# Twenty places instead of eighteen for the expert weights of a hybrid-attention and mixture-of-experts block

## What is computed

```python
h = x
h = h + hybrid_mixer(rms_norm(h, norm_mix_g), w_in, q_norm_g, k_norm_g, w_proj_a, w_proj_b, w_out, cos, sin)
hn = rms_norm(h, norm_ffn_g)
h = h + moe_ffn(hn, w_router, b_router, w_gate_up, b_gate_up, w_down, b_down)

# moe_ffn: 32 experts, the 4 best of a token by the router's logits, gates = softmax over these 4;
# for each expert e and the tokens xb that chose it:
hgu = xb @ w_gu[e] + b_gu[e]                          # 1024 x 2048
gate, up = min(hgu[:, :1024], 7), clip(hgu[:, 1024:], -7, 7)
y = ((up + 1) * gate * sigmoid(1.702 * gate)) @ w_down[e] + b_down[e]   # 1024 x 1024
```

## Time and profile before

| | |
|---|---|
| median of 3 runs | 1224.87 us (1224.17 to 1225.32) |
| the profiled execution's own time | 1224.58 us |
| span of its trace | 1223.0 us |
| PE busy | 1146.1 us, 94% |
| DMA queue of SP | 434.83 MB, 87.9% of 16 DMA engines over the span |
| DVE, ACT, POOL busy | 23%, 9%, 3% |

### The profile page before, as it was taken

One profiled execution on the slowest core, in us unless ns is written; L12 is line 12 of the kernel. 1 busy time (PEld: TensorE's weight loads), 2 busy tenths in 40 slices (PEclk: granted clock), 3 DMA queues, 4 the chain that ended last, 5 costly groups with the idle time before them and its releaser, 6 DMA issues.

```text
span 1223.0 us, 12848 instructions
## 1 busy us (share of the span) xinstructions
PE 1146.1 (94%) x5681; PEld 553.6 (45%) x5681; DVE 277.8 (23%) x590; ACT 113.1 (9%) x206; POOL 33.0 (3%) x23
## 2 busy tenths in 40 slices
PE   6959999979999999999999978999999999999996
PEld 3656878554444444444444324444443333333331
DVE  1297332332111112221111111211111111111111
ACT  1102542010000000000000000000000000000000
POOL 1170000000000000000000000000000000000000
PEclk9979999968999999999999997999999999999999
DMA  7535336367999999999999999999999999999994
GB/s 231 168 138 216 129 138 275 142 275 292 373 418 417 417 418 416 418 417 417 417 417 417 417 417 417 416 418 417 417 417 417 417 417 417 416 417 417 417 417 199
DMA packets 87560, 435.75 MB, mean 356 GB/s; under 512 B 8688, under 2 KB 9872, under 8 KB 54640
## 3 DMA queue, kind: packets, MB, share of 16 engines
q1 hardware_dynamic: 87376, 434.83, 87.9%
q0 software_dynamic: 96, 0.08, 0.2%
q10 hardware_dynamic: 32, 0.01, 0.0%
HBM read 433.84 MB, written 1.05 MB: 356 GB/s over the span
## 4 chain that ended last, share of the span: by engine, by line
PE 63%; DMA 25%; DVE 4%; SPq 3%; issue 2%; ACT 1%; POOL 0%; DVEq 0%; POOLq 0%
PE Pp L682 25%; DMA ring<-in_w_gate_up 16%; PE Bp L697 12%; PE Bp L669 7%; DMA qkv<-in_w_gate_up 6%; PE Pp L456 5%; PE Pp L444 4%; PE Ap L711 3%; SPq L317 3%; PE Pp L609 2%; DMA XT<-in_w_gate_up 2%; PE Ap L620 1%; PE Pp L676 1%; PE Bp L689 1%; DVE ring L891 1%
## 5 line engine op out<-in xcount | busy, mean ns | idle before, releaser
L682 PE MATMUL Pp<-ring,OBT 128*64 128x512 f32 x1360 | 308.9, 603 | 14.4 <-DMA ring<-in_w_gate_up 14.4
L682 PEld LDWEIGHTS Pp<-ring,OBT 128*64 128x64 f32 x1360 | 95.6, 138 | 214.3 <-issue 166.0
L1086 DVE TENSOR_SCALAR G<-Pp 128x512 f32<-128x512 f32 x32 | 22.1, 691 | 674.1 <-PE Pp L682 674.1
L697 PE MATMUL Bp<-ring,G 128*64 128x512 f32 x688 | 152.8, 596 | 0.9 <-DVE G L1097 0.9
L669 PEld LDWEIGHTS Bp<-cst,XR 128*128 128x128 f32 x1024 | 122.6, 199 | 31.0 <-issue 31.0
L669 PE MATMUL Bp<-cst,XR 128*128 128x64 f32 x1024 | 127.2, 285 | 5.4 <-issue 4.4
L697 PEld LDWEIGHTS Bp<-ring,G 128*64 128x64 f32 x688 | 47.5, 137 | 90.7 <-issue 89.7
L456 PE MATMUL Pp<-XT,unit 128*128 128x256 f32 x384 | 85.9, 383 | 0.0
L682 PE MATMUL Pp<-unit,OBT 128*64 128x512 f32 x352 | 78.9, 594 | 2.5 <-DMA unit<-in_w_gate_up 2.4
L456 PEld LDWEIGHTS Pp<-XT,unit 128*128 128x128 f32 x384 | 72.7, 192 | 11.0 <-issue 1.1
L697 PE MATMUL Bp<-unit,G 128*64 128x512 f32 x320 | 70.9, 595 | 0.0
(11 more groups left out here) (191 smaller groups left out, 673.8 us busy)
## 6 DMA issues: line engine op xcount, KB each, us to landing
ring<-in_w_gate_up SPq DMA_DIRECT2D x170, 1024.0 KB, 20.7
ring<-in_w_down SPq DMA_DIRECT2D x86, 1024.0 KB, 25.4
unit<-in_w_gate_up SPq DMA_DIRECT2D x44, 1024.0 KB, 21.2
unit<-in_w_down SPq DMA_DIRECT2D x40, 1024.0 KB, 24.8
qkv<-in_w_gate_up SPq DMA_DIRECT2D x21, 1024.0 KB, 21.0
XT<-in_w_gate_up SPq DMA_DIRECT2D x21, 1024.0 KB, 19.2
unit<-in_w_in SPq DMA_DIRECT2D x8, 2048.0 KB, 7.9
ring<-in_w_out SPq DMA_DIRECT2D x2, 2048.0 KB, 12.9
```

The source lines that it names most:

```text
L682: last = mm((Gps, Ups)[q // 2][64 * (q % 2):64 * (q % 2) + 64, :], xT[:, k, :], w[:, q * 512:(q + 1) * 512], start=False, stop=k == KC - 1 ...
L697: last = mm(Yps[64 * hf:64 * hf + 64, :], hT[:, k % 4, k // 4, :], w[:, half * 1024 + hf * 512:][:, 0:512], start=k == 0, stop=k == KC - 1 ...
L1086: V.tensor_scalar(gm, Gps, LIMIT, None, ALU.min).then_inc(d_gm, 1)
```

## The change

`PLACES` goes from 18 to 20, so every piece from turn 18 on sits in another place, and `load_after_release` waits for the piece 20 turns ahead. Pieces 8 and 9 of expert 1, which have turns 18 and 19, now have places that nothing used before; they are issued during the mixer, right behind units 8 and 9.

```diff
-PLACES = 18
+PLACES = 20
...
         unit = sb("unit", [P, 2, 4096])
+        more = sb("more", [P, 2, 2048])
...
-            qkv[:, 0:2048], XT[:, :, :].rearrange("p k t -> p (k t)")]
+            qkv[:, 0:2048], XT[:, :, :].rearrange("p k t -> p (k t)"), more[:, 0, :], more[:, 1, :]]
...
                 if u >= 5 and u < 8:
                     load_unit(u + 6)
+                if u >= 8 and u < 10:
+                    load_piece(1, u)
...
-            for s in range(8, PIECES):
+            for s in range(10, PIECES):
                 load_after_release(1, s)
...
-    nc = bacc.Bacc("TRN2", target_bir_lowering=False, num_devices=1)
+    nc = bacc.Bacc("TRN2", target_bir_lowering=False, num_devices=1, dynamic_dma_scratch_size=2048)
```

More of the change, by code:

```diff
@@ L298, in load_unit, with load_piece @@
                     sp.dma_start(dst, src).then_inc(unit_in[u], 16)
+            def load_piece(e, s):
+                at, full, _ = place_of(e, s)
+                dst = at if s < 8 else at.rearrange("p (k n) -> p k n", k=2)
+                sp.dma_start(dst, piece_src(e, s)).then_inc(full, 16)
             for u in range(11):
```

## The result

The changed kernel takes 1218.12 us in the median of 6 runs (1216.52 to 1220.11), beside 1224.81 us of the kernel before: a ratio of 0.9944, 95% interval 0.9931 to 0.9957. That is 6.7 us less where 5.0 us were forecast, and 0.2 us under the low end of the stated range. Two more sets of 5 runs beside the kernel before gave 1219.49 us (0.9956, 0.9942 to 0.9969) and 1219.40 us (0.9963, 0.9950 to 0.9975). The forecast, 1219.8 us against 1224.87 us, is a ratio of 0.9959.

A forecast was written before the change was run, and what follows sets the result against it. The prediction took saturated DMA, through the last gate piece's landing, as the bound: 1224.58 us less 5.0 us for two pieces, all other terms 0, gave 1219.6 us, or 1219.8 us as median. The range was 1218.3 to 1222.0 us.

The forecast's parts named there:

- What bounds the kernel: The end hangs on the landing of piece 7 of expert 31, set by DMA saturated at 417 GB/s.
- Two landings, 5.0 us: In the experts every piece is there two landings earlier, 2 x 2.515 = 5.03 us, taken as 5.0.
- So the n-th landing after the first release comes when it came before, but it is the piece two further on: Between 281.7 and 340 us releases at the old times leave the same 5.8 us of DMA idle time.
- two pieces leave the saturated stretch: 22 pieces are issued before the first release and 362 after it, where 364 were left; worth 5.0 us.
- Where it shows: Expert 14's waits gone, 1.2 us of wait left in expert 15, break 5.0 us earlier, last part 24.2 us as before.
- the start of the experts: First issue after a release stays at 281.70 us, though its chain of small steps may shift by a few tenths.
- a first release that moves: One of the signs that the prediction is wrong; the first issue after a release was expected at 281.7 us.
- The scratch: POOL's three small DMAs at the head: cost taken as 0, upper bound 6.9 us late.
- SP's stream: Two issues of 0.33 us each stand earlier in the mixer, two fewer in the experts: 0.
- the units' cover: Mixer units 9 and 10 land 17 and 12 us before PE needs them, so the early loads cost 0.
- none of the four: Rivals: scratch too small (0.05); lead worth nothing or half (0.07); more than two pieces (0.02); mixer units late (0.01).
- 1 and 4: POOL late from small scratch, 1226.8 or 1234 us, chance 0.05; units 9 or 10 late, at worst 1225 us, chance 0.01.

The follow-up runs named there:

- e1_scratch: The kernel before with the DMA scratch cut to 2048 bytes alone, 18 places: 1224.51 us in 11 runs, ratio 0.9997.
- e3_own: Against the kernel before: two pieces loaded early in the mixer into places of their own, the rest rotating over 18; 1223.18 us, ratio 0.9987.
- r_after2: The changed kernel a third time, no edit, against the kernel before: 1219.40 us, ratio 0.9963.
- e4_again: The changed kernel with 22 places in rotation, run again beside the change on one chip: 1217.47 us, ratio 0.9943.
- e2_late: The changed kernel with the two early pieces issued behind piece 7 of expert 1 instead of in the mixer: 1219.68 us, ratio 0.9956.
- r_after: The changed kernel again, no edit, on another chip with another trace: 1219.49 us, ratio 0.9956 to the kernel before.
- e8_warm2: The changed kernel with fifteen added PE products that nothing reads, to hold the clock: 1215.00 us, ratio 0.9922.
- e9_22warm2: The kernel with 22 places plus the same fifteen added products that nothing reads: 1210.91 us in 4 runs, ratio 0.9890.
- e4_22: The changed kernel with 22 places, att and the rear of G joining the rotation, first time: 1218.31 us, ratio 0.9947.

## Why the prediction was right in the mechanism and off in the number

- *What bounds the kernel:* right. The end follows the last gate piece's landing, and that follows DMA: in the traces of e1_scratch and the change, with equal starts, landing and span differ by 5.07 and 5.0 us.
- *Two landings, 5.0 us:* right in size. Traces with equal starts give 5.07 us, one chip's medians 5.0 us (1224.40 to 1219.40); by all 16 runs of the change (median 1219.0 us, worked out over the three sets) it is some 5.4 to 5.9 us against the medians of before (1224.40 to 1224.85). The 6.7 us of the first set are thus in part luck: the two later sets, 1219.49 and 1219.40 us, lie 0.3 and 0.4 us from the forecast. What the last 0.4 to 0.9 us over the 5.0 us are, no run shows.
- *"So the n-th landing after the first release comes when it came before, but it is the piece two further on":* right for the change, but its heading, that two pieces leave the saturated stretch, names only half of the reason. With the two pieces early and no deeper rotation 1.7 us are gained, with the rotation and nothing early 4.2 us. What carries the gain is two more pieces that may be under way or waiting at any time; the early loads let it begin with both landed.
- *Where it shows:* right. Expert 14 without a wait in the chain, a landing in expert 15 still waited for, the break and the last part unchanged but for the clock.
- *The step that failed is the start of the experts, put at a shift of nothing:* "the first release hangs on a chain of small steps at half of PE's clock that may shift by a few tenths", and "the runs of before spread by -0.7 and +0.5 us". The prediction named a first release that moves as a sign of being wrong, and it moved: by 1.2 us, and expert 1's first product by 2.0 us. Of the 2.0 us, 0.6 us are there when the router begins (248.85 and 248.28 us), 0.7 us come in the chain of small steps (32.85 and 32.2 us) and 0.7 us in expert 0, where the clock comes back later in the trace of before. So the chain shifts by little more than the few tenths; left out was what lies ahead of it and behind it. Over the eleven traces the router begins anywhere from 247.10 us (e3_own) to 250.63 us (r_after2), the first issue after a release starts anywhere from 279.95 us (e3_own) to 283.39 us (e4_again), and the stretch behind the last gate landing takes 22.4 to 25.5 us. The end goes with PE's granted clock, and of the mixer's share up to 3 us goes with the pace of its first products; the rest of it (e3_own begins the router 1.2 us ahead of the change after the same 19.39 us for these) stays open. The spread of three runs was also taken for the spread of the kernel: in 22 runs the kernel before took 1222.04 to 1227.20 us. A range of +-2.5 us about the same middle, the spread of single executions, would have held all three medians.
- *The scratch, SP's stream, the units' cover:* right at 0, as e1_scratch, PE's rows at 176.63 and 192.31 us, and e2_late show. The Trainium skill ("SBUF — State Buffer", SBUF size: 192, 224, or 256?) has 16 KiB as set aside for GpSimd's descriptors; with three DMAs of 80 KB in all, 2 KB did the same work here.
- *The rivals:* none of the four came; for 1 and 4 the point above has the rows. The rate stayed at 417 GB/s with two destinations more.

## What to carry to other kernels

Where a transfer queue is saturated to the end, count the landings between its first saturated moment and the one that the end hangs on; each buffer more in the rotation takes at most one landing off that count, while the queue is still short of releases (two more took off 5.0 us here, the next two about 2 us); where the queue never rests, nothing more is to be expected of it. Look for buffers that one early use sets apart, since they rotate for free, and test depth and early loading separately: they look like one change and are not. Before you state a range for a change of a few us, compare several traces of the same program at three or four fixed points, from the first products on: a delay near 20 us moves the end just as one near 280 us does. Where the clock falls in idle waits, consider filling them.

## What the runs showed of the hardware that was not expected

The pace of PE differs between executions of one program. At the head of the mixer the products run at half pace until about 22 us in r_after and at full pace throughout in the change's first trace, and the granted clock does not show it (1.00 in both). Ahead of the experts the granted clock fell to half (1.2 of 2.4 GHz) at about 250 to 255 us, where PE stands idle for 2.1 and then 5.0 us between narrow products, and came back between 280 and 285 us, while PE was in expert 0's wide products. With products of 128x512 in the waits it stayed up (e8_warm2, e9_22warm2). That the moments differ by execution is shown; why they differ is not.

DMA's landings are not even when the queue is full. In the trace of e4_22 two pieces in a row land at 313.14 and 317.26 us (304.34 + 8.8 and 306.06 + 11.2), 4.1 us apart, although three more were issued behind them by 311.7 us, and this is the DMA view of 313 to 318 us:

```profile
q1 hardware_dynamic: 529, 2.04, 101.4%
q8 instruction: 1, 0.02, 1.4%
```

The page of before has 46 such packets with 0.75 MB, 16.3 KB each. One takes about 1.1 us of one DMA engine (1.4% of 16 engines over 5 us). The Trainium skill ("Runtime: NRT & Kernel Launch", Instruction fetch mechanics) says that instructions are fetched in blocks of 16 KiB by DMA, and the size in this trace agrees. That these blocks make the difference of 1 to 2 us between the landings of otherwise equal traces (885.6 to 887.5 us behind expert 1's first product in those of the change and of e2_late) is an argument from where they stand in time; no run here takes them away, and none shows how the time of one engine holds up a whole piece.
